# Gated FFN up projections as 2x2 block products: seven products per pair of weight tiles instead of eight

## What is computed

```python
def swiglu(x, w_in, w_out):          # x 512x1024, w_in 1024x5632, w_out 2816x1024
    gate, up = jnp.split(x @ w_in, 2, axis=-1)
    return (jax.nn.silu(gate) * up) @ w_out

for l in range(2):
    x = x + 0.5 * rms_norm(swiglu(rms_norm(x, g1), w_ffn1_in[l], w_ffn1_out[l]), g2)
    x = x + rms_norm(token_mixing(rms_norm(x, g3), ...), g4)
    x = x + 0.5 * rms_norm(swiglu(rms_norm(x, g5), w_ffn2_in[l], w_ffn2_out[l]), g6)
    gate = jax.nn.sigmoid(rms_norm(x, g7) @ w_ple_gate[l])
    x = x + rms_norm(gate * (p[l] @ w_ple_proj[l]), g8)
# then the second block: attention and an FFN with a convolution
```

## Time and profile before

| | |
|---|---|
| median of three runs | 2898.39 us |
| profiled execution: span from its first to its last instruction | 2896.7 us |
| TensorE busy | 2846.7 us, 98% |
| VectorE busy | 1379.2 us, 48% |
| ScalarE busy | 1141.2 us, 39% |
| GpSimd busy | 15.7 us, 1% |
| granted TensorE clock | 0.997 of full |

### The profile page before, as it was taken

One profiled execution on the slowest core, in us unless ns is written; L12 is line 12 of the kernel. 1 busy time (PEld: TensorE's weight loads), 2 busy tenths in 40 slices (PEclk: granted clock), 3 DMA queues, 4 the chain that ended last, 5 costly groups with the idle time before them and its releaser, 6 DMA issues. The chain is left out here.

```text
span 2896.7 us, 41108 instructions
## 1 busy us (share of the span) xinstructions
PE 2846.7 (98%) x17248; PEld 2402.4 (83%) x17248; DVE 1379.2 (48%) x1923; ACT 1141.2 (39%) x1655; POOL 15.7 (1%) x29
## 2 busy tenths in 40 slices
PE   8999999999999999999999999999999999999998
PEld 7888888878888888888888877888888888888887
DVE  3334355676333355333336667333346258756541
ACT  3223244554232245222235555223236357544430
POOL 0000000000000000000000000000000000000000
PEclk9999999999999999999999999999999999999999
DMA  4233412103223431223412103122332111222331
GB/s 152 96 101 126 142 39 66 39 3 117 87 95 109 138 117 52 92 97 107 149 49 79 53 4 110 61 100 95 132 122 95 59 49 33 102 73 96 101 124 51
DMA packets 71415, 254.32 MB, mean 88 GB/s; under 512 B 8056, under 2 KB 9080, under 8 KB 71232
## 3 DMA queue, kind: packets, MB, share of 16 engines
q1 hardware_dynamic: 71232, 251.70, 25.9%
HBM read 249.57 MB, written 2.10 MB: 87 GB/s over the span
## 5 line engine op out<-in xcount | busy, mean ns | idle before, releaser
L214 PE MATMUL ps<-h_hi,w_space 128*128 128x512 f32 (+1 forms) x5056 | 1445.8, 370 | 3.0 <-DVE h_lo L312 3.0
L214 PEld LDWEIGHTS ps<-h_hi,w_space 128*128 128x128 f32 x5056 | 919.1, 189 | 163.8 <-DVE h_lo L312 3.8
L202 DVE TENSOR_TENSOR w_space<-w_raw,w_space 128x1024 fp32r<-128x1024 f32 x440 | 533.5, 1223 | 1015.7 <-ACT w_space L195 1015.6
L214 PE MATMUL ps<-h_lo,w_space 128*128 128x512 f32 (+1 forms) x2528 | 930.9, 368 | 0.0
L195 ACT CAST w_space<-w_raw 128x1024 fp32r<-128x1024 f32 x440 | 455.8, 1048 | 898.9 <-PE ps L214 551.1
L224 PE MATMUL ps<-w_space 128*128 128x512 f32 x3216 | 737.3, 390 | 1.3 <-PEq L91 0.8
L224 PEld LDWEIGHTS ps<-w_space 128*128 128x128 f32 x3216 | 602.0, 188 | 125.9 <-issue 1.2
L214 PEld LDWEIGHTS ps<-h_lo,w_space 128*128 128x128 f32 x2528 | 477.9, 189 | 77.5 <-issue 0.5
L607 ACT CAST w_space<-act_p 128x512 fp32r<-128x512 f32 x88 | 54.7, 621 | 186.1 <-DVE act_p L619 186.1
L622 DVE TENSOR_TENSOR w_space<-act_p,w_space 128x512 fp32r<-128x512 f32 x88 | 60.9, 692 | 60.5 <-ACT w_space L607 60.5
L619 DVE TENSOR_TENSOR act_p<-act_s,ps 128x512 f32<-128x512 f32 x88 | 59.9, 680 | 54.9 <-PE ps L214 54.9
(11 more groups left out here) (412 smaller groups left out, 2195.5 us busy)
## 6 DMA issues: line engine op xcount, KB each, us to landing
w_raw<-in_w_ffn_in SPq DMA_DIRECT2D x176, 512.0 KB, 3.4
w_raw<-in_w_ffn_out SPq DMA_DIRECT2D x88, 512.0 KB, 3.5
w_raw<-in_w_in SPq DMA_DIRECT2D x64, 512.0 KB, 3.4
w_raw<-in_w_up SPq DMA_DIRECT2D x44, 512.0 KB, 3.4
w_raw<-in_w_out SPq DMA_DIRECT2D x24, 512.0 KB, 4.0
w_raw<-in_w_down SPq DMA_DIRECT2D x22, 512.0 KB, 3.5
w_raw<-in_w_ple_gate SPq DMA_DIRECT2D x16, 512.0 KB, 3.5
gain_pre<-in_gains_pre SPq DMA_DIRECT2D x10, 512.0 KB, 4.8
```

What stands on the lines that cost most here:

```text
L202: nc.vector.tensor_tensor(self.lo(n), self.raw[:, n % SLOTS, :], self.hi(n).bitcast(F32), ALU.subtract).then_inc(self.lo_ready, 1)
L214: m = nc.tensor.matmul(c.ps[:, bank, t], part[:, cols], moving[:, k, t], start=(k == 0 and i == 0), stop=(k == KD - 1 and i == 2))
```

## The change

For pairs 3 to 21 of each of the four gated FFNs the 256-wide product of a gate tile and an up tile (together: weights 1024 x 256, tokens 512) is seen as a 2x2 block product: the features in two halves of 512, the tokens in two halves of 256, the outputs in gate and up. It is computed in the form of Strassen and Winograd with seven block products:

- weight sides: the blocks a11 (gate, first half of the features) and a12 (gate, second half) as loaded, a22 (up, second half), and four sums: s1 = a21 + a22, s2 = s1 - a11, s3 = a11 - a21, s4 = a12 - s2, where a21 is up, first half. GpSimd makes s1 and s3 (`sums_early`, `sums_late`, first halves; L813, L817), VectorE s2 and s4 (L1005, L1012).
- token sides: b11, b21, b22 are blocks of h; t1 = b12 - b11, t2 = b22 - t1, t3 = b22 - b12, t4 = b21 - t2. They are made once per FFN: GpSimd adds hi and lo of the four blocks (L805), VectorE subtracts. t3 takes the place of b12 in h.
- seven products m1 to m7, each 4 blocks x 3 parts = 12 matmuls of 256 columns. Their sums are made in PSUM: ScalarE copies m1 into the other bank before m6 is added there ("seeded", L944), keeps m5 aside ("kept", L947) and later the sum with m6 ("carried", L956); VectorE adds twice in PSUM (L1058, L1066).

Further differences that follow from it: each pair has one gate and one up load with a release of its own (`add_raw`); the three weight operands of 1024 are cast by ScalarE and their remainders made by VectorE (`part_hi`, `part_lo`, L901 and L986), a22 is one of 512. The up product stays whole in `cells` until the down phase and is split there in a ring of four (`act_hi`, `act_lo`, `scalar_down`, `vector_down`). Down rows use five slots in turn (`ROW_SLOTS`). One weight operand lies where the gains lie (`w_extra`), so SP loads the gains after the last m6 (`wait_extra`). In the blocks that begin with an `ffn1`, SP now loads all 22 down rows before the gains and the mask.

```diff
+CELL_SLOTS = (6, 0, 7, 4, 2)
+HALF_SLOT = 5
+T_SLOTS = (9, 10, 8)
+X_SLOTS, LATE_SLOT = ((11, 12), (1, None)), 3
+ROW_SLOTS = (12, 1, 11, 3, 8)
+PLAIN = 3
...
+    def load_to(self, sp, end):
+        last = self.units[end - 1].load + 1
+        while self.loaded < last:
+            i = self.loaded
+            if i >= SLOTS:
+                freed, count = self.loads[i - SLOTS].freed
+                sp.wait_ge(freed, count)
...
+            self.gate[q] = c.W.add_raw(w_in[2 * q], (c.seven_rested, self.rested_no["s", q, 4]))
+            self.up[q] = c.W.add_raw(w_in[2 * q + 1], (c.seven_rested, self.rested_no["x", q, 3]))
...
+    def gpsimd(self, pool, nc):
...
+        for q in range(PLAIN, KF):
+            gate, up = W.raw_of(self.gate[q]), W.raw_of(self.up[q])
+            W.wait_loaded(pool, self.up[q])
+            if q > PLAIN:
+                self.wait_rested(pool, "s", q - 1, 4)
+            nc.gpsimd.tensor_tensor(c.sums_early[:, 0:S], up[:, 0:S], up[:, S:D], ALU.add).then_inc(c.made, 1)
+            W.wait_loaded(pool, self.gate[q])
+            if q > PLAIN:
+                self.wait_rested(pool, "x", q - 1, 2)
+            nc.gpsimd.tensor_tensor(c.sums_late[:, 0:S], gate[:, 0:S], up[:, 0:S], ALU.subtract).then_inc(c.made, 1)
...
+        for k in range(HALF_K):
+            cols = slice(k * P, (k + 1) * P)
+            for i, (part, moving) in enumerate(((x_hi, t_hi), (x_hi, t_lo), (x_lo, t_hi))):
+                m = nc.tensor.matmul(out, part[:, cols], moving[:, k, :], start=(name == "m1" and k == 0 and i == 0),
+                                     stop=(k == HALF_K - 1 and i == 2), skip_group_check=(name != "m1"))
+        m.then_inc(c.seven_done, 1)
+
+    def tensor_rest(self, pe, nc):
...
+        for q in range(PLAIN, KF):
+            if q > PLAIN:
+                pe.wait_ge(c.silu_ready, self.f0 + q - 3)
+            self.wait_rested(pe, "x", q, 0)
+            self.tensor_product(pe, nc, q, "m1")
+            self.wait_rested(pe, "x", q, 1)
+            self.tensor_product(pe, nc, q, "m5")
+            if q > PLAIN:
+                self.wait_rested(pe, "x", q - 1, 3)
+                self.wait_rested(pe, "d", q - 1)
+                self.tensor_product(pe, nc, q - 1, "m4")
+            self.wait_split(pe, "seeded", q)
+            self.tensor_product(pe, nc, q, "m6")
+            self.wait_split(pe, "kept", q)
+            self.tensor_product(pe, nc, q, "m2")
+            self.wait_split(pe, "carried", q)
+            self.wait_rested(pe, "x", q, 2)
+            self.tensor_product(pe, nc, q, "m7")
+            self.wait_rested(pe, "c", q)
+            self.tensor_product(pe, nc, q, "m3")
...
+    def act_hi(self, act, nc, k):
+        c = self.c
+        act.wait_ge(c.product, self.f0 + k + 1)
+        if k < 4:
+            act.wait_ge(c.seven_done, self.done_no(LAST, ("m5", "m6")[k // 2]))
+        else:
+            act.wait_ge(c.W.done, self.down.d0 + k - 3)
+        nc.scalar.copy(self.act_parts(k)[0], self.cell(k)).then_inc(c.act_hi, 1)
...
+        self.silu(act, nc, 2)
+        act.wait_ge(W.done, self.u0 + 2 * PLAIN)
+        self.t_hi(act, nc, "t3")
+        self.wait_rested(act, "t3")
...
+    def scalar_down(self, act, nc):
+        for k in range(4, KF):
+            self.act_hi(act, nc, k)
+            self.c.W.hi_to(act, nc, self.down.d0 + k + 1)
...
             def _(sp):
                 start.load(sp)
-                c.W.load_to(sp, ffn.down.d0 + SLOTS)
+                c.W.load_to(sp, ffn.down.d0 + KF)
+                ffn.wait_extra(sp)
                 proj.turn.load(sp)
                 attention.load(sp, ffn)
                 c.W.load_to(sp, proj.u0 + 12)
```

## The result

| us | before | after |
|---|---|---|
| median, measured side by side (20 runs each) | 2899.58 | 2903.68 |
| span of the profiled execution | 2896.7 | 2901.0 |
| TensorE busy | 2846.7 | 2799.1 |
| TensorE waiting for the tokens of a next stage | 17.2 | 61.1 |
| granted TensorE clock | 0.997 | 0.989 |

The ratio after to before is 1.0014, 95% interval 1.0008 to 1.002: a little slower, less than the 0.2% that I had called the limit of a clear change. I had forecast 2884.

A forecast was written before the change was run, and what follows sets the result against it. TensorE, busy 2846.7 of 2896.7 us, was taken as the bound. Terms -62.7 + 0.5 + 8.2 + 34.5 + 2.5 + 2.3 = -14.7 us of span gave 2884; own range 2875 to 2892, whole range 2866 to 2918.

The forecast's parts named there:

- Products: 76 FFN pairs: 84 matmuls of 256 columns take 10.05 us against 10.87 before; -62.7 us.
- late landings: Weight loads in the product pairs that land late: 0.03 us a pair, +2.3 us in all.
- Rivals 1 (the ring): Product pairs: the loop of up weights, GpSimd and VectorE binds, slower than 10.05 us a pair; 2916 us; chance 0.20.
- 4 (no gain): Products: 256-column matmuls or bank changes cost more than 0.1197 us, so no gain; 2944 us; chance 0.04.
- Join: From plain tiles to products, TensorE waits 2.05 us for the seed copy; four FFNs, +8.2 us.
- Tails: FFN ends: next stage's transposes 9.95 us late before mix projection, 7.3 before gate, two each; +34.5 us.
- Rival 2 (the tails hide): FFN ends: half of the 34.5 us is saved, weights landing before ScalarE wants them; 2867 us; chance 0.09.
- Port: Stage start: GpSimd's four sums of 1024 hold VectorE ahead of transposes TensorE waits for; +2.5 us, up to 10.
- rival 3: GpSimd and VectorE with two SBUF inputs exclude each other fully: +7.5 us on the forecast, 2891 us; chance 0.20.
- seed: One additional seeding matmul per FFN, 0.12 us each in four FFNs; +0.5 us.

The follow-up runs named there:

- 8: Changed kernel with all four weight sums of a pair on VectorE, GpSimd doing only the sums of h; 2904.4 us.
- Experiments 3 to 5: 3: changed kernel, mask load behind first six weight units, 2894.8 us; 4: that plus casts spread in the turn, 2856.8; 5: casts spread, mask first, 2873.1.
- 9: Kernel of experiment 4 with GpSimd's four sums of h waiting until VectorE has made the tokens of all four quarters; 2853.1 us.
- experiments 1 and 2: 1: changed kernel, TensorE repeats matmuls in tail holes, 2895.2 us; 2: kernel before, ScalarE does extra squares ahead of its first norm, 2948.3 us.
- experiment 4: Changed kernel with the mask load behind the first six weight units and the next stage's casts and remainders spread in the turn; 2856.8 us.
- 11: The very kernel of experiment 4 run again, on a different chip; 2861.7 us.

## Why the prediction was wrong

It forecast a gain of 14.7 us of span; there was a loss of 4.3. The 19 us stand in these terms:

- **Products:** right. -62.7 and +2.3 for late landings were forecast, -60 came, and no group of waits inside the pairs is in the list of TensorE's waits. Rivals 1 (the ring) and 4 (no gain) are refuted, by the 10.08 us and by 8, which puts more on VectorE's part of the ring.
- **Join:** 8.2 forecast, 7.3 came. What I left out is the clock behind it.
- **Tails:** the mechanism was right (the first projection unit is cast 5.7 us after the tail's start, computed 5.8); the size was not. 34.5 forecast, 40.4 came: the table load ended 1.5 us later than computed at the first tail, as units 4 and 5 land later, and the holes before the gate were 8.5 and 8.9 us, not 7.3. Experiments 3 to 5 show that this term is made of the mask's place and the casts' place. Rival 2 (the tails hide) is refuted.
- **Port:** 2.5 forecast, about 3.5 came (3.6 by what 9 gives back at its four places, half clock left out), at the place named (GpSimd's sums of h beside the tokens) and in the third FFN. The durations there, 3.08 us for 1.28, show the exclusion of rival 3; its price, 10 us, did not come, since in the pairs and most turns TensorE does not wait for what is held up. By this the trace agrees with the rule of the Trainium skill that the prediction names.
- **The step that failed:** the tails, computed as 9.95 and 7.3 us late, were booked in the sum at just that. A hole on TensorE costs its length and the half clock behind it, 2.0 to 2.75 us at each tail (9.3) and about 1.5 at those joins where it fell (3). That term, 12 of the 19 us, is nowhere in the sum, and experiments 1 and 2 show it by itself: taken away it gave 7 to 8.5 us back, added to the kernel before it cost 8.4 beside the holes (7 by the medians, 10 by the spans). The other 6 are the tails' size and 1 the port.

My bounds for the tails reached 17 us down but only 3 up. The whole range, 2866 to 2918, held the time by luck: its upper end was there for the ring, which never bound. The range of the forecast itself, 2875 to 2892, did not hold it.

Open: the terms of experiment 4 (products -60, seed 0.5, joins 7.3, waits for tokens 22.7 - 17.2 = 5.5) make -46.7, and its span is only 41.8 below the one before. Of the 5 us between, some 1.4 are half clock in the first mixing stage (granted clock 0.83 at 553 to 559 us) and 1.5 behind the hole shown under experiment 4; 1.5 go the other way, as the half clock of the kernel before at 2361 to 2366 us is missing. The rest, some 3.5 us, lies in pieces of 0.1 to 0.9 us beside waits at the heads of stages and was not taken apart. Why a hole of 1.8 us brings the half clock in one profile and not in another was not tried either.

## To carry to other kernels

A change that saves on the bounding engine everywhere and puts holes into a few seams has to be priced at the seams, with the clock behind each hole: here four holes of 9 to 13 us and the half clock behind them ate 50 of the 60 us saved, and the joins and their half clock another 10. Look at what stands in order ahead of the first operation of the next stage, on the engine that casts and on the queue that loads; moving four casts back at each seam, and one DMA at two of them, turned a loss of 4 us into a gain of 44. And engine contention should be looked for where the held-up engine is the one waited for, not where it is largest.

## What the runs showed of the hardware

- TensorE's granted clock had fallen to half (1.2 of 2.4 GHz) after holes of 5.4 us and more in every tail looked at, and behind holes of 1.8 to 2.0 us in some profiles only (four of four joins in 11, two of four in the changed kernel, none in 4). Behind a tail 8 transposes took 1.97 us instead of 1.09; behind a join it cost 1.5 us.
- Over the twenty executions of the changed kernel the time goes with the mean granted clock: 2899.9 and 2900.1 us at 0.991, 2906.3 to 2907.3 us at 0.987.
- GpSimd and VectorE with two SBUF inputs side by side: GpSimd 3.3 us for 1024 columns, 2.4 alone; VectorE 3.08 to 3.43 at the first turn for 1.22 to 1.28 alone; an addition of GpSimd over 8 columns, 0.25 us by itself, lasted 1.05 behind VectorE. VectorE's h_lo, which reads PSUM, kept its 1.22 us beside GpSimd (experiment 9).
